# Sixteen modulation slots on GpSimd: scaled and summed over eight chunks there, then added over partitions by TensorE

## The chip, the cores and the metric

The kernel runs on one core of a Trainium2 chip. The metric is the device time of one execution in microseconds (us). Three runs of the kernel before gave 1271.75, 1271.87 and 1272.66 us; the median is 1271.87.

## What is computed

A sequence of 256 tokens with 1024 channels passes two adaptive-norm layers (an "even" mixer with two kinds of attention, an "odd" mixer with banded attention), then two layers of a second block with four mixers and a feed-forward part. The change touches only the modulation of the first two layers:

```
cs = silu(c)                                   # 1024 numbers
for layer in range(2):
    mod = cs @ ada_w[layer] + ada_b[layer]     # 1024 x 3072 matrix
    shift, scale, gate = split(mod, 3)
    h = rms_norm(x, norm_g[layer]) * (1 + scale) + shift
    y = even_mixer(h, ...) if layer == 0 else odd_mixer(h, ...)
    x = x + gate * y
```

So mod is a product of one vector with a matrix of 12.6 MB a layer. Shift and scale of layer 0 are needed before anything else, its gate at the end of the even mixer, shift and scale of layer 1 behind that, and its gate at the end of the odd mixer.

## The kernel before

All weights come as slots of 128 partitions x 2048 float32 (1 MB). NAMES (line 77 on) lists the 200 slots in the order in which TensorE works on them. A ring of four buffers takes most slots, three more buffers in big2 take the modulation slots (line 114 on). SP issues all loads in the order of LOADS (line 138), each behind a wait until the slot that used its buffer before is done (line 1048 on). The transfers that come first are the head: eight modulation slots ada0_0 to ada0_7, for shift and scale of layer 0.

An ordinary slot is a projection of 1024 channels to 256. Its float32 weights are split in two parts: ScalarE copies the rounded high part (L740), VectorE subtracts it (L749, 128x2048, both inputs in SBUF), and TensorE makes three sets of 16 products with them, the third of them with the low part.

A modulation slot (names with "ada") holds 4 chunks of 128 input channels by 512 output channels. TensorE multiplies its 128x128 blocks as the moving operand with cs spread over 32 columns as the stationary one: 16 products a slot, 32 for a pair of slots that shares a PSUM bank. VectorE then picks the columns with four masked reductions (L1887) into mod_raw. Sixteen of the 24 modulation slots come behind the head.

The attention of a layer runs in steps k, with two score maps a step. In each step TensorE makes the scores of pair k, the value products of pair k - 2, the transposes of pair k - 1, and then the slots that the table FILL (line 44) names for that step, whose products keep TensorE occupied while the softmax is made. VectorE adds the bias tables in L578, normalises in L603 (L600 for the second map of a differential head, with two SBUF inputs), subtracts low parts of weights (L749) and of the attention's output (L514), and takes projections out of PSUM. Step 8 and the tail have no scores. Before the change the pairs of modulation slots stand in FILL at steps 0, 2, 3, 5, 8 and the tail of the even layer, in ODD_GATE behind even_out3, and at step 6 of the odd layer.

GpSimd sets some constants at the start and is then idle until the second block (line 2714 on). All instructions of an engine run in its program's order, so a wait of an instruction holds all behind it.

## Time and profile before

| | value |
|---|---|
| median of three runs | 1271.87 us |
| span of the profiled execution, first to last instruction | 1269.9 us |
| TensorE busy | 1245.3 us, 98% |
| VectorE busy | 826.1 us, 65% |
| ScalarE busy | 683.2 us, 54% |
| GpSimd busy | 94.1 us, 7% |
| granted TensorE clock, mean | 0.999 |
| even attention, its eight score steps | 72.2 to 147.2 us |

The profile is that of one execution, recorded in hardware; all times of rows are counted from the start of its span. The span leaves out what lies around the first and the last instruction, so it is 2.0 us below the median of the runs. Busy shares are means over stages with different limits, so single stages are read below.

### The profile page before, as it was taken

What the parts mean: (1) busy time and instruction counts of PE and PEld (TensorE: products, weight loads), DVE (VectorE), ACT (ScalarE), POOL (GpSimd) and SP (SyncE); (2) the same over time, 40 slices, a digit from 0 to 9 for tenths busy, and PEclk for the clock granted to TensorE, in tenths of its full rate; (3) what the DMA queues carried; (4) which work ended last, traced back from release to release, by engine and by line L of the source; (5) the groups of instructions that cost most, each with busy time, mean ns of one, the idle gap of its engine ahead of it and who ended that gap; (6) DMA issues with size and microseconds to landing.
All of it is one profiled execution on the core that took longest, in us unless ns stands there. A gap on an engine that the chain in (4) does not pass through costs nothing.

```text
span 1269.9 us, 24768 instructions
## 1 busy us (share of the span) xinstructions
PE 1245.3 (98%) x10488; PEld 1125.1 (89%) x10488; DVE 826.1 (65%) x1251; ACT 683.2 (54%) x885; POOL 94.1 (7%) x79
## 2 busy tenths in 40 slices
PE   6999999999999999999999999999999999999997
PEld 5998899889999999999888888999999999888886
DVE  3667766886866869766655545766868866655442
ACT  2556446865856567245544435856567345544433
POOL 0000000000001330230000000000330230000000
PEclk9999999999999999999999999999999999999999
DMA  9867665624434433235454554434433225555452
GB/s 386 302 256 271 258 233 197 252 92 167 166 134 166 166 134 133 70 105 195 168 197 170 195 198 167 167 133 167 166 134 109 93 100 189 192 170 195 166 191 75
DMA packets 35102, 222.93 MB, mean 176 GB/s; under 512 B 3888, under 2 KB 8240, under 8 KB 9264
## 3 DMA queue, kind: packets, MB, share of 16 engines
q1 hardware_dynamic: 31248, 216.23, 47.8%
q10 hardware_dynamic: 3744, 5.11, 1.2%
q8 instruction: 83, 1.36, 0.4%
q14 instruction: 27, 0.22, 0.1%
HBM read 220.28 MB, written 1.05 MB: 174 GB/s over the span
## 4 chain that ended last, share of the span: by engine, by line
PE 88%; DVE 5%; ACT 3%; DMA 2%; issue 1%; SPq 0%; ACTq 0%; DVEq 0%
PE pj L635 58%; PE yv L635 14%; PE sc L635 10%; PE tp L635 4%; DVE ring_rounded L749 3%; PE tp L501 1%; DMA ring<-weights 1%; PE tp L1998 1%; ACT w_split L740 1%; DMA xT<-x_t 1%; DVE att_area L578 1%; ACT att_area L532 0%; DVE scr_rounded L2694 0%; DVE xT L1026 0%; ACT hT L2479 0%
## 5 line engine op out<-in xcount | busy, mean ns | idle before, releaser
L749 DVE TENSOR_TENSOR ring_rounded<-ring,w_split 128x2048 fp32r<-128x2048 f32 x106 | 248.5, 2350 | 59.5 <-ACT w_split L740 57.4
L2224 DVE TENSOR_TENSOR ring_rounded<-ring,big_rounded 128x2048 fp32r<-128x2048 f32 x66 | 151.3, 2293 | 107.1 <-ACT big_rounded L2095 107.0
L740 ACT CAST w_split<-ring 128x2048 fp32r<-128x2048 f32 x106 | 202.2, 1907 | 32.1 <-PE pj L635 22.5
L635 PE MATMUL pj<-h_split,w_split 128*128 128x256 f32 x1264 | 172.4, 286 | 0.2 <-ACT w_split L2474 0.2
L635 PE MATMUL pj<-h_split,ring_rounded 128*128 128x256 f32 x1264 | 165.2, 281 | 1.3 <-DVE ring_rounded L749 1.2
L635 PEld LDWEIGHTS pj<-h_split,w_split 128*128 128x128 f32 x1264 | 156.1, 188 | 7.1 <-issue 5.1
L635 PEld LDWEIGHTS pj<-h_split,ring_rounded 128*128 128x128 f32 x1264 | 155.7, 188 | 2.9 <-DVE ring_rounded L749 2.1
L2095 ACT CAST big_rounded<-ring 128x2048 fp32r<-128x2048 f32 x66 | 126.2, 1912 | 49.9 <-PE pj L635 48.3
L635 PE MATMUL pj<-hT_rounded,w_split 128*128 128x256 f32 x1136 | 146.0, 280 | 0.0
L635 PEld LDWEIGHTS pj<-hT_rounded,w_split 128*128 128x128 f32 x1136 | 139.2, 188 | 0.0
L635 PE MATMUL sc<-big_rounded 128*128 128x512 f32 x176 | 68.8, 391 | 0.0
L635 PE MATMUL pj<-big_rounded 128*128 128x512 f32 x176 | 68.5, 389 | 0.0
L1420 POOL TENSOR_TENSOR big<-big 128x512 f32<-128x512 f32 x16 | 30.7, 1920 | 467.6 <-DVE big L1337 459.4
L2324 ACT ACTIVATE big<-pj 128x512 f32<-128x512 f32 x32 | 19.1, 598 | 70.5 <-PE pj L635 70.4
L532 ACT ACTIVATE att_area<-att_area,stat 128x256 f32<-128x256 f32 (+1 forms) x80 | 39.9, 499 | 19.4 <-DVE stat L578 8.3
L2104 ACT CAST big_rounded<-tp 128x512 fp32r<-128x512 f32 x22 | 12.9, 586 | 68.8 <-PE tp L1998 68.8
L635 PE MATMUL yv<-big_rounded,yT_rounded 128*128 128x512 f32 x192 | 49.2, 398 | 0.1
L635 PE MATMUL yv<-big_rounded,rw_rounded 128*128 128x512 f32 x192 | 47.7, 390 | 0.0
L635 PE MATMUL yv<-ring_rounded,yT_rounded 128*128 128x512 f32 x192 | 47.5, 389 | 0.0
L635 PEld LDWEIGHTS yv<-ring_rounded,yT_rounded 128*128 128x128 f32 x192 | 36.0, 188 | 7.5
L635 PEld LDWEIGHTS yv<-big_rounded,rw_rounded 128*128 128x128 f32 x192 | 35.9, 188 | 7.4
L635 PEld LDWEIGHTS yv<-big_rounded,yT_rounded 128*128 128x128 f32 x192 | 35.0, 188 | 8.2 <-issue 0.8
(377 smaller groups left out, 2120.0 us busy)
## 6 DMA issues: line engine op xcount, KB each, us to landing
ring<-weights SPq DMA_DIRECT2D x180, 1024.0 KB, 4.8
big<-weights SPq DMA_DIRECT2D x20, 1024.0 KB, 7.5
first_block<-biases ACTq DMA_DIRECT2D x26, 192.0 KB, 4.4
first_block<-biases SPq DMA_DIRECT2D x6, 192.0 KB, 10.6
xT<-x_t SPq DMA_DIRECT2D x1, 1024.0 KB, 9.3
out_t<-scr SPq DMA_DIRECT2D x4, 256.0 KB, 2.9
con<-constants SPq DMA_DIRECT2D x1, 897.0 KB, 6.5
aux<-small SPq DMA_DIRECT2D x1, 832.0 KB, 10.3
```

What stands on the lines that cost most here:

```text
L501: last = nc.tensor.transpose(tp[m["t"] % 2][:, at:at + P], probs[:, m["g"] % 4, it, jt * P:(jt + 1) * P], C("ident"))
L532: ins = nc.scalar.activation(pr, pr, ACT.Exp, bias=st[:, it:it + 1], scale=-1.0, accum_out=st[:, 2 + it:3 + it])
L578: ins = nc.vector.tensor_tensor_reduce(probs[:, m["g"] % 4, it, 0:size], sc[m["g"] % 2][:, it * SEQ:it * SEQ + size], table[:, P - it * P: ...
L635: return nc.tensor.matmul(out, lhsT, rhs, start=start, stop=stop, skip_group_check=True)
L740: act.post(nc.scalar.copy(w_split[:, w % 2], ring[:, in_ring(idx)]), s["w_high"])
L749: dve.post(nc.vector.tensor_tensor(ring_r[:, at], ring[:, at], w_split[:, w % 2].bitcast(F32), ALU.subtract), s["w_low"])
L1420: pool.tell(nc.gpsimd.tensor_tensor(d, b, b[:, :, n - 1:n].to_broadcast([P, 512 // (2 * n), 2 * n]), ALU.subtract), s["hgrn_diff"])
L1998: last = nc.tensor.transpose(tp[j % 2][:, (2 * c + T) * P:(2 * c + T + 1) * P], by_token(j, T)[:, c * P:(c + 1) * P], C("ident"))
L2095: act.tell(nc.scalar.copy(w_high(i), ring[:, in_ring(w_at(t, i))]), s["ffn_high"])
L2104: act.tell(nc.scalar.copy(hidden_high(j), tp[j % 2][:, :]), s["ffn_placed"])
L2224: dve.tell(nc.vector.tensor_tensor(w_low(t, i), w, value(w_high(i)), ALU.subtract), s["ffn_low"])
L2324: free(act, nc.scalar.activation(GATES[name], b[:, :], ACT.Tanh, scale=0.5), name)
```

## The change

The sixteen slots behind the head no longer go through TensorE as weights. Their layout is changed so that a half slot of 1 MB holds 4 chunks of input channels, with the 512 output channels in order. GpSimd multiplies each chunk (128x512) by its column of cs, and adds the chunks of two half slots in raw, an area that is otherwise used in the second block only. TensorE adds the result over partitions: four products with a 128x128 block of the sum as the stationary operand and one column of ones as the moving one. VectorE copies the four columns out of PSUM. The eight results are called mod0_4, mod0_5, mod1_0 to mod1_5, and stand at other places of FILL than the pairs did. They are no weight slots any more: SP issues their loads behind the streamed weight slots that MOD_AFTER counts, from the fourth on, into the same three buffers, behind a wait on mod_read for the half slot that had the buffer. The sums go round over four places of raw.

```diff
-    "even": {-1: ["even5"], 0: ["even6", "ada0_8", "ada0_9"], 1: ["even8"], 2: ["even13", "ada0_10", "ada0_11"],
-             3: ["even7", "ada1_4", "ada1_5"], 4: ["even9"], 5: ["even10", "ada1_6", "ada1_7"], 6: ["even11"], 7: ["even14"],
-             8: ["ada1_0", "ada1_1"], 9: ["even15"], EVEN_TAIL: ["ada1_2", "ada1_3"]},
-    "odd": {0: ["odd1"], 1: ["odd6"], 2: ["odd2"], 3: ["odd7"], 4: ["odd3"], 5: ["odd8"], 6: ["ada1_10", "ada1_11"],
+    "even": {-1: ["even5"], 0: ["even6"], 1: ["even8", "mod0_4"], 2: ["even13"], 3: ["even7", "mod0_5"], 4: ["even9"],
+             5: ["even10", "mod1_0"], 6: ["even11", "mod1_1"], 7: ["even14"], 8: ["mod1_2"], 9: ["even15"],
+             EVEN_TAIL: ["mod1_3"]},
+    "odd": {0: ["odd1"], 1: ["odd6"], 2: ["odd2"], 3: ["odd7"], 4: ["odd3"], 5: ["odd8"], 6: ["mod1_5"],
             7: ["odd9"]},
-ODD_GATE = ("ada1_8", "ada1_9")
+ODD_GATE = ("mod1_4",)
+MODS = [n for n in NAMES if "mod" in n]
+MOD_AFTER = (3, 4, 6, 7, 8, 9, 10, 11, 12, 13, 14, 15, 17, 18, 19, 20)
+def mod_buffer(j):
+    return RING + (j + 1) % OWN
+        def mod_sum(n):
+            return raw[:, 2 * (n % 4):2 * (n % 4) + 2, 1:SEQ + 1]
+            streamed = [i for i in LOADS if i >= len(HEAD_BUFFERS)]
+            mods_behind = {}
+            for j, n in enumerate(MOD_AFTER):
+                mods_behind.setdefault(streamed[n], []).append(j)
-                sp.dma_start(weights(i), w_d[i]).then_inc(landed[b], 16)
+                sp.dma_start(weights(i), w_d[ROW[i]]).then_inc(landed[b], 16)
+                for j in mods_behind.get(i, ()):
+                    if j < OWN:
+                        before, _ = head_use[mod_buffer(j)]
+                        sp.wait_ge(slot_done, before + 1)
+                    else:
+                        sp.wait_ge(s["mod_read"].sem, j - OWN + 1)
+                    sp.dma_start(mod_weights(j), mod_d[j]).then_inc(landed[mod_buffer(j)], 16)
+        def dve_mod_columns(dve, name):
+            b = done(dve, name)
+            at = 4 * int(name[-1])
+            free(dve, nc.vector.tensor_copy(mod_raw[:, at:at + 4], b[:, 0:4]), name)
+        def pe_mod(pe, name):
+            n = MODS.index(name)
+            use = bank_use(name)
+            pe.eng.wait_ge(bank_free[use % NPJ], use // NPJ)
+            pe.eng.wait_ge(s["mod_read"].sem, 2 * n + 2)
+            for m in range(4):
+                last = matmul(bank_of(name)[:, m:m + 1], mod_sum(n)[:, m // 2, (m % 2) * P:(m % 2 + 1) * P],
+                              C("ones")[:, 0:1], m == 0)
+            last.then_inc(slot_done, 1)
+        def pool_mods(pool):
+            pool.eng.wait_ge(s["cond_ready"].sem, 1)
+            for n, name in enumerate(MODS):
+                if n >= 4:
+                    pool.eng.wait_ge(slot_done, IDX[MODS[n - 4]] + 1)
+                total = mod_sum(n)
+                for half in range(2):
+                    j = 2 * n + half
+                    _, head_uses = head_use[mod_buffer(j)]
+                    pool.eng.wait_ge(landed[mod_buffer(j)], 16 * (head_uses + j // OWN + 1))
+                    w = [mod_weights(j)[:, 2 * k * SEQ:(2 * k + 2) * SEQ] for k in range(4)]
+                    for k in range(4):
+                        ins = nc.gpsimd.tensor_scalar(w[k], w[k], cs[:, 4 * half + k:4 * half + k + 1], None, ALU.mult)
+                    pool.do(ins)
+                    terms = [k.rearrange("p (m t) -> p m t", t=SEQ) for k in w]
+                    if half:
+                        terms = [total] + terms
+                    for k in range(1, len(terms)):
+                        ins = nc.gpsimd.tensor_tensor(total, terms[0] if k == 1 else total, terms[k], ALU.add)
+                        if k < len(terms) - 1:
+                            pool.do(ins)
+                    pool.tell(ins, s["mod_read"])
...
             pool.tell(nc.gpsimd.memset(eps[:, 1:2], 64e-5), s["constants_set"])
+            pool_mods(pool)
             eng.wait_ge(rest_landed, 48)
```

## Rows read from the trace of the kernel before

**Rows 1.** The page, busy time, share of the span and instructions.
```profile
PE 1245.3 (98%) x10488; PEld 1125.1 (89%) x10488; DVE 826.1 (65%) x1251; ACT 683.2 (54%) x885; POOL 94.1 (7%) x79
```

**Rows 2.** The page, shares by engine of the chain that ended last.
```profile
PE 88%; DVE 5%; ACT 3%; DMA 2%; issue 1%; SPq 0%; ACTq 0%; DVEq 0%
```

**Rows 3.** Stretches: length, busy PE, PEld, DVE, ACT, POOL, granted clock, DMA; even steps.
```profile
81.60:89.40 7.80, 7.80 (x68) 7.27 (x64) 6.47 (x23) 4.43 (x11) 0.00 (x0) 1.00 0.97 377
...
129.90:138.20 8.30, 8.30 (x68) 7.65 (x64) 7.42 (x26) 3.58 (x11) 0.00 (x0) 1.00 0.98 379
...
sum 75.00, PE 74.65 PEld 67.17 DVE 57.41 ACT 45.94 POOL 0.00; mean PE 9.33 PEld 8.40 DVE 7.18 ACT 5.74 POOL 0.00
```

**Rows 4.** TensorE in order of time: start, us, line, output and inputs, count, wait before.
```profile
41.70 2.15 PE L635 MATMUL pj<-h_split,ring_rounded 128*128 128x256 f32 x16
...
79.75 1.95 PE L635 MATMUL pj<-big,cs 128*32 128x128 f32 x64
81.63 1.13 PE L635 MATMUL sc<-big 64*128 64x256 f32 x8
...
150.30 1.13 PE L635 MATMUL yv<-probsT,big 128*128 128x256 f32 x4 [0.58 <-ACT probsT L547]
...
189.03 0.50 PE L635 MATMUL tp<-con,rstd 128*128 128x1 f32 x4
189.39 0.91 PE L635 MATMUL sc<-con 128*128 128x128 f32 x6
...
267.55 1.08 PE L635 MATMUL yv<-probsT,big 128*64 128x256 f32 x8 [0.99 <-ACT probsT L547]
```

**Rows 5.** VectorE in order of time, first layer.
```profile
39.35 2.29 DVE L749 TENSOR_TENSOR ring_rounded<-ring,w_split 128x2048 fp32r<-128x2048 f32 x1
...
131.15 0.42 DVE L578 CUSTOM_DVE_ANT_0 att_area<-sc,first_block 128x256 f32<-128x256 f32 x1
...
139.47 0.42 DVE L578 CUSTOM_DVE_ANT_0 att_area<-sc,first_block 128x256 f32<-128x256 f32 x1 [0.28 <-DVE big L1862]
...
190.12 0.19 DVE L1887 CUSTOM_DVE_ANT_0 diag<-pj,con 128x32 f32<-128x32 f32 x1
...
190.36 0.19 DVE L1887 CUSTOM_DVE_ANT_0 diag<-pj,con 128x32 f32<-128x32 f32 x1
```

**Rows 6.** VectorE by source line: least, median and most ns of one.
```profile
L603 DVE TENSOR_SCALAR att_area<-att_area,stat x72: 285/354/357, 77.7 to 870.5; 128x256 f32<-128x256 f32 x64, 128x128 f32<-128x128 f32 x8
```

**Rows 7.** GpSimd in order of time, second block.
```profile
429.27 0.99 POOL L1435 TENSOR_TENSOR big<-big 128x256 f32<-128x256 f32 x1 [6.07 <-issue]
430.34 1.43 POOL L1420 TENSOR_TENSOR big<-big 128x512 f32<-128x512 f32 x1
...
445.69 2.98 POOL L1420 TENSOR_TENSOR big<-big 128x512 f32<-128x512 f32 x1
```

**Rows 8.** VectorE in order of time, the same stretch.
```profile
416.22 0.69 DVE L1689 TENSOR_TENSOR big<-raw 128x512 f32<-128x512 f32 x1
...
429.70 1.11 DVE L1689 TENSOR_TENSOR big<-raw 128x512 f32<-128x512 f32 x1
430.85 1.73 DVE L1691 SCALAR_TENSOR_TENSOR raw<-big,vec,raw 128x256 f32<-128x256 f32 x2
...
445.06 2.71 DVE L749 TENSOR_TENSOR ring_rounded<-ring,w_split 128x2048 fp32r<-128x2048 f32 x1
447.69 1.26 DVE L1367 COPY vfirst<-raw 128x512 f32<-128x512 f32 x1
```

**Rows 9.** GpSimd by source line: least, median and most ns of one.
```profile
L1970 POOL TENSOR_TENSOR big<-big x16: 1263/1277/3220, 535.8 to 1023.6; 128x512 f32<-128x512 f32 x16
...
L1407 POOL CAST att_area_rounded<-con x8: 293/368/462, 282.7 to 549.9; 128x128 fp32r<-128x128 f32 x8
```

**Rows 10.** SP's queue in order of time: the issue of loads.
```profile
21.01 6.39 SPq L1058 DMA_DIRECT2D ring<-weights  x4
...
99.73 0.43 SPq L1058 DMA_DIRECT2D ring<-weights  x1
```

More of the change, by code:

```diff
@@ L105, in is_split @@
 def is_split(name):
-    return not any(part in name for part in ("ada", "branch1", "ffn", "down"))
+    return not any(part in name for part in ("ada", "mod", "branch1", "ffn", "down"))
 SPLIT = [i for i, n in enumerate(NAMES) if is_split(n)]
@@ L136 @@
 BUFFERS = buffers()
+ROW = {i: row for row, i in enumerate(i for i, b in enumerate(BUFFERS) if b)}
 EARLY_BY = 6
-LOADS = sorted(range(len(NAMES)), key=lambda i: (max(BUFFERS[i][2], i - EARLY_BY if i >= len(HEAD_BUFFERS) else -1), i))
+LOADS = sorted((i for i, b in enumerate(BUFFERS) if b),
+               key=lambda i: (max(BUFFERS[i][2], i - EARLY_BY if i >= len(HEAD_BUFFERS) else -1), i))
 in_ring = lambda idx: BUFFERS[idx][0]
@@ L632, in weights, with mod_weights @@
             return ring[:, b] if b < RING else big2[:, (b - RING + 1) * SLOT:(b - RING + 2) * SLOT]
+        head_use = {}
+        for i_, b_ in enumerate(HEAD_BUFFERS[:BUFFERS.index(None)]):
+            head_use[b_] = (i_, BUFFERS[i_][1])
+        def mod_weights(j):
+            at = (mod_buffer(j) - RING + 1) * SLOT
+            return big2[:, at:at + SLOT]
+        def mod_sum(n):
+            return raw[:, 2 * (n % 4):2 * (n % 4) + 2, 1:SEQ + 1]
         def matmul(out, lhsT, rhs, start=True, stop=True):
@@ L2309, in act_slot @@
                 act_diff_root(act)
-            if "ada" not in name:
+            if "ada" not in name and name not in MODS:
                 act_highs(act, split_beyond(name.split(".")[0],
@@ L2329, in dve_slot @@
         def dve_slot(dve, name):
-            if "." not in name and "ada" not in name:
+            if "." not in name and "ada" not in name and name not in MODS:
                 dve_lows(dve, split_beyond(name, 1))
@@ L2334, in dve_evacuate @@
         def dve_evacuate(dve, name):
-            if "ada" in name:
+            if name in MODS:
+                dve_mod_columns(dve, name)
+            elif "ada" in name:
                 if ada_part(name) % 2:
@@ L2767, in pack_weights @@
         for n in range(4):
-            out[IDX[f"{t}branch{n}"]] = a["w_branch_2"][layer, n].reshape(2, P, D).transpose(1, 0, 2).reshape(P, SLOT)
+            out[ROW[IDX[f"{t}branch{n}"]]] = a["w_branch_2"][layer, n].reshape(2, P, D).transpose(1, 0, 2).reshape(P, SLOT)
         put(a["w_out_2"][layer], numbered(t + "out", 4))
@@ L2773, in pack_weights, with pack_modulations @@
         for i in range(FC):
-            out[IDX[f"{t}ffn{i}"]] = slots[i]
+            out[ROW[IDX[f"{t}ffn{i}"]]] = slots[i]
         slots = a["w_ffn_down_2"][layer].reshape(FC // 2, 2, P, D).transpose(0, 2, 1, 3).reshape(FC // 2, P, SLOT)
         for i in range(FC // 2):
-            out[IDX[f"{t}down{i}"]] = slots[i]
+            out[ROW[IDX[f"{t}down{i}"]]] = slots[i]
     return out
+def pack_modulations(a):
+    parts = np.stack([a["ada_w"][layer].reshape(2, 4, P, 6, 4 * P).transpose(3, 0, 2, 1, 4).reshape(6, 2, P, SLOT)
+                      for layer in range(2)])
+    return np.concatenate([parts[int(n[3]), int(n[-1])] for n in MODS])
 def pack_vectors(a):
@@ L2819 @@
         "weights": pack_weights(a),
+        "modulations": pack_modulations(a),
         "vectors": pack_vectors(a),
```

23 lines of the change are left out of this document (13 added, 10 removed).

## The prediction

> **What bounds the kernel now.** I read the shares of the span by engine first, then the chain of work that ended last, then single stretches. TensorE is busy for 98% of the span, GpSimd for 7% [rows 1], and the chain of waits names TensorE for 88% of its length [rows 2]. So time that leaves TensorE is worth its full length, if the engine behind it is not late. The table by attention step of the even layer says where that holds: TensorE is full at full clock, VectorE works 6.47 of 7.80 us in an early step and 7.42 of 8.30 in a later one, in all eight steps 57.41 of 75.00 us [rows 3]. In that later step its first instruction starts at 131.15, and the next step's at 139.47 after an idle time of 0.28 us that an instruction of VectorE itself ended [rows 5]: 8.04 us of work in a step of 8.3 of TensorE's. VectorE is the second bound, 0.3 us below the first.
>
> **What is removed.** A pair of modulation slots is 32 products, twice the 16 of a slot: the row "x64" at 79.75 counts their two passes and spans 1.95 us, 1.88 net of the overlap with the next row, which starts at 81.63 [rows 4]. Eight such pairs go. Not each is worth 1.88 us:
> - Behind even6, even13, even7 and even10 TensorE has no wait after the pair. Four times 1.88 = 7.5 us. The pair at the tail of the even attention: 1.9 us.
> - The pair of step 8 (from 147.8 to 149.7) is followed by the product over probsT at 150.30, which waited for ScalarE [rows 4]. Only this cover goes, so 0.
> - The pair behind even_out3 lies beside the residual and the squares that its successors need anyway, so 0 on TensorE. On VectorE four masked reductions stand from 190.12 on ahead of the scaled norm, at a pitch of 0.235 us [rows 5]: 0.94 us, for one copy of four columns instead, which I put at 0.2 (one reduction on 32 columns takes 0.19). 0.75 us.
> - In the odd attention TensorE waits 0.99 us for ScalarE soon after the pair, at 267.55 [rows 4]. Again VectorE's 0.75 counts.
> Sum 10.9 us.
>
> **What is added on TensorE.** Four products of one column a pair. The nearest row, four of 128x1 at 189.03, spans 0.50, 0.36 net of its successor at 189.39 [rows 4]. Five of the eight lie on the path: 1.8 us; the others fall into the waits above. Net 9.1 us saved, if nothing else happens.
>
> **What is added on GpSimd.** Sixteen half slots of four tensor_scalar 128x512 and three or four adds 128x512. An add takes 1.277 us in the median and 1.263 at least [rows 9], with its wait on the one before about 1.36. A tensor_scalar of that size is in no row. From below: a cast of a quarter of the columns takes 0.293 at least [rows 9], so not less than that. From above: the add, 1.28, which reads two inputs. I take 0.65: half of the add, one input being half of two, and between a cast's least time and twice its median of 0.368. A half slot is then 4 x 0.65 + 3.5 x 1.36 = 7.4 us, all 118 us.
>
> The Trainium skill, "GPSIMD Engine Reference", section "When to use GPSIMD", says that two-input elementwise work there is about half as fast as on VectorE and one-input work near line rate. The trace agrees on the first, 1.277 us against VectorE's 0.69, and no run here shows the second. By that page the tensor_scalar would take about what VectorE takes for an operation of 512 columns, 0.69, and the sum would stand; it speaks against rival 2.
>
> **What GpSimd does to VectorE.** This decides. At 429.27 GpSimd starts a tensor_tensor of 0.99 us, at 429.70 VectorE one of 128x512 with both inputs in SBUF. It takes 1.11 us instead of the 0.69 of the same line at 416.22, so it ends at 430.81. GpSimd's next (430.34) ends at 431.77, and the two VectorE instructions behind take 1.73 instead of 1.0 [rows 7, 8]. At 445.69 GpSimd's lasts 2.98, across a split subtraction that itself lasts 2.71 for 2.29; then the copy of SBUF to SBUF, 128x512, lasts 1.26 [rows 7, 8]. So the two engines exclude each other for whole instructions and take turns. The wait of VectorE behind a waiting GpSimd add is 0.75 us, since 0.3 of the add's 1.27 passes before it needs the turn. Behind a tensor_scalar of 0.65 it would be 0.2 to 0.25. With a gap of 0.2 us in between both lose 0.2. A mean over the mix (half and half) is 0.5 back to back, 0.33 behind a gap, and 0.38 for an instruction that meets GpSimd at a random point.
>
> Which VectorE instructions count? Subtractions of split weights (L749), those at L600, L514 and L1016 have two SBUF inputs. The normalisation at L603 has one: 0.354 us for 128x256 [rows 6], below the 0.42 of L578 for the same size, which reads PSUM [rows 5], so it runs in a faster mode. That the copy at 447.69, which has one SBUF input too, was held speaks for counting it, and I do.
>
> Rule by rule: the Trainium skill, "SBUF — State Buffer", section "SBUF: two separate sides", says that VectorE and GpSimd share one port pair as an exclusive lock that is held for an instruction, and that a VectorE instruction takes it with two SBUF inputs or in a two-port mode. The rows at 429 to 448 agree, 1.11 for 0.69 us. By the rule L603 counts.
>
> Without L603 the waits of the eight steps, summed below, are 4 x 0.4 + 4 x 1.8 = 8.8 instead of 19.2 us and fit into VectorE's idle time but for 1.5; with 2.5 at the start and 1 behind, 5.0 us are lost and the time would be 1268. That is the other end of this choice.
>
> **Is GpSimd busy when VectorE needs the turn?** The first of its loads stands behind even1's, and the four ring loads with even1's among them are issued between 21.0 and 27.4 us [rows 10], so it lands near 34. From then a half slot arrives with about every streamed weight slot, every 6 to 10 us. With one turn of 2.0 us for L749 and short ones for the rest, a half slot takes 9.6 us. So GpSimd stays behind its loads and works without a pause until about 150 us. TensorE's deadlines hold: half slot 11 is done at about 150, and mod1_3 stands at 151 plus what VectorE loses. On SP's queue a load of a half slot waits for mod_read (the one three before is read), and the weight slots behind it wait too, some up to 10 us: even10's is issued at 99.73 [rows 10] and its products start at 122.1, once the step's other products behind 119.6 are done, 22 us of cover, so no loss. Were GpSimd slower, both covers would be gone, see the rivals.
>
> **The sum of the waits.**
> - Start: from 34 to 42 us the first half slot meets eight L2604 and the L749 of 39.35, which ends at 41.64. TensorE takes its result at 41.70 [rows 4, 5], so all waits ahead of it count: five turns, about 2.5 us.
> - The eight steps: an early step (0 to 3) has L749 and four L603, 0.38 + 0.33 + 0.5 + 0.33 + 0.5 = 2.0 us of waits; a later one (4 to 7) L749, two L603, one small tensor_scalar, two L600 and one L514, 2.8 us. Together 4 x 2.0 + 4 x 2.8 = 19.2. VectorE's own time is 57.4 [rows 3] less 4 x 0.75 for the reductions, and 0.03 us between each of some 170 instructions, 5 us: 59.5. With the waits 78.7. TensorE needs 75.0 - 4 x 1.88 + 4 x 0.36 = 68.9. Excess 9.8 us. About 0.7 of the idle time lies where it can't be used, and 2.0 are made good behind step 7, where VectorE has less to do. 8.5.
> - Behind the attention: the last four half slots end near 187 us, beside L749, L514 and L2616, three turns: 1.5. The eight L1016, from 194 us on, are just clear.
>
> Sum 12.5 us. With the 9.1 saved that is +3.4. The profiled span is 1269.9 and the median of the runs 1271.87, so 2.0 us lie around the span: 1273.3 and 2.0, forecast 1275.3.
>
> **The rivals.**
> 1. The waits find idle time. For it: VectorE idles 1.3 us of 7.8 early [rows 3], the score and probability buffers are two and four deep, and no row shows a tensor_scalar held. Against: the 0.28 us of idle time [rows 5]. At its full size 9.1 us stay saved, 1263; without L603 it is the 1268 above.
> 2. GpSimd is slow (slower than before clearly): its tensor_scalar costs as much as an add, 1.28. A half slot is 10.2, with its turns 12.6 us; the turns cost VectorE 3.3 and 4.3 instead of 2.0 and 2.8 a step, 30.4 over the eight, so 19.7 are lost there, 3.5 at the start and 2 behind: 25.2 in place of 12.5, 1288. From about 1.1 us a tensor_scalar on, half slot 11 (180 us) also misses mod1_3 (171), where TensorE stands in order with even_out behind it: 9 us more, 1297. For it: the cast of only 128 columns takes up to 0.46 [rows 9]. Against: its least, 0.293.
> 3. The loads: a mod_read wait on SP holds even10 to even15 back until ScalarE's split is late. Each half slot over 10 us adds its excess, five times 2, so 1285. Against: the 22 us of cover [rows 10].
>
> **Chances.** The forecast 0.43, with its own range 1269 to 1283; rival 1 0.28; rival 2 0.23; rival 3 0.05; 0.01 for something unseen. Within 0.2% (2.5 us, about what a measurement of this kernel tells from no change) lies 0.16 of the forecast's 0.43 and 0.01 of rival 1; 0.27 of rival 1 is faster, and 0.01 of the forecast. Faster 0.28, same 0.17, slower 0.55 with rivals 2 and 3. Range 1262 to 1293: all of rival 1, and two thirds of rival 2.
>
> **What would show it.** L749 in 75 to 150 us with a mean over 2.5 instead of 2.29 us, and L603, L600 above 0.5: right. L603 at 0.354 beside a busy GpSimd: wrong in its count. GpSimd's tensor_scalar near 0.65 us, its last add before 190 us. An interval between two score products of steps 5 to 7 of over 9.5 us: VectorE is the bound. TensorE idle before mod1_3 because of GpSimd: rival 2. Granted clock still 1.00, as in rows 3. If the attention steps shrink by 1.5 us each where a pair left, the forecast is wrong and rival 1 right.

## The result, and the profile after

The changed kernel takes 1314.51 us in the median of 4 runs (1314.33 to 1315.61), the kernel before, on the same chip, 1272.05. The ratio is 1.0337, with a 95% interval of 1.0325 to 1.0349: 42.5 us slower, where 3.4 slower was forecast and 1293 was the upper end of the range. The profiled execution took 1315.6 us, its span 1313.6. Line numbers moved, those that are read here mostly by 11 to 23: L658 is TensorE's product (L635 before), L772 the subtraction of split weights (L749), L614 the normalisation (L603), L611, L525 and L1039 were L600, L514 and L1016, L763 is ScalarE's split (L740 before).

The page of the kernel after, its busy times, the slices for GpSimd and the granted clock, and the chain that ended last; they answer to [rows 1, 2]:

```profile
PE 1253.7 (95%) x10040; PEld 1132.5 (86%) x10040; DVE 836.6 (64%) x1195; ACT 682.5 (52%) x885; POOL 297.4 (23%) x199
...
POOL 0799999500000231150000000000330230000000
PEclk9998869999999999999999999999999999999999
...
PE 79%; POOL 11%; DVE 3%; DMA 2%; ACT 2%; issue 1%; SPq 0%; ACTq 0%; POOLq 0%; DVEq 0%
```

GpSimd is now 11% of the chain, where it had no entry. It works without a pause from 40.8 to 250 us, and within that time, from about 100 to 200 us, TensorE's granted clock falls (each digit of these two lines is a slice of 33 us, in tenths). The stretches say where the time went. In each row: length, busy PE, PEld, DVE, ACT, POOL, granted clock, DMA share and rate. First the kernel before: from the first to the eighth score product of the even attention, its end and tail, even_out, the norm with the first odd projections.

```profile
72.20:138.20 66.00, 65.65 (x725) 58.82 (x724) 49.40 (x151) 40.46 (x82) 0.00 (x0) 1.00 0.69 265
138.20:160.00 21.80, 21.22 (x265) 19.28 (x264) 16.50 (x36) 11.69 (x21) 0.00 (x0) 1.00 0.63 241
160.00:185.80 25.80, 25.80 (x224) 25.08 (x219) 14.92 (x32) 12.28 (x13) 0.00 (x0) 1.00 0.62 237
185.80:209.50 23.70, 23.70 (x252) 22.87 (x251) 17.40 (x31) 11.39 (x16) 0.00 (x0) 1.00 0.46 162
```

The same four stretches of the kernel after:

```profile
72.80:150.60 77.80, 66.39 (x503) 59.21 (x502) 56.48 (x120) 39.85 (x82) 75.53 (x47) 0.91 0.56 199
150.60:197.30 46.70, 24.85 (x153) 22.20 (x152) 18.34 (x32) 13.64 (x22) 45.19 (x31) 0.70 0.56 211
197.30:225.50 28.20, 28.20 (x218) 27.66 (x218) 16.86 (x24) 10.29 (x11) 27.44 (x17) 0.90 0.47 184
225.50:249.80 24.30, 23.03 (x196) 22.19 (x194) 17.70 (x24) 11.39 (x16) 23.64 (x13) 1.00 0.44 157
```

The losses are 11.8, 24.9, 2.4 and 0.6 us; 0.6 came before the first of these stretches, and 0.6 in the odd attention and the projections behind it. That is 41.0 of the 43.7 us by which the spans differ. The other 2.7 come in the second block, where both kernels do the same: 0.5 by 400 us of the kernel before, 0.9 near 515 and 1.4 near 1000 us; why is open. In the second stretch TensorE is busy for 24.85 of 46.70 us, so 21.3 of the 24.9 lost are waits; the other 3.6 are longer busy time, with fewer products than before, at a granted clock of 0.70. TensorE in order of time, with the wait before an instruction in brackets, to set beside [rows 4]:

```profile
107.59 0.95 PE L658 MATMUL pj<-con,raw 128*128 128x1 f32 x8
...
112.82 1.97 PE L658 MATMUL yv<-probsT,big 128*64 128x256 f32 x8 [3.22 <-ACT probsT L558]
...
140.44 2.04 PE L658 MATMUL yv<-probsT,big 128*128 128x256 f32 x4 [4.84 <-DVE big L1896]
...
161.81 1.88 PE L658 MATMUL yv<-probsT,big 128*128 128x256 f32 x4 [2.96 <-ACT probsT L558]
...
171.66 1.84 PE L658 MATMUL pj<-con,raw 128*128 128x1 f32 x8 [7.12 <-POOL raw L1963]
...
174.85 3.98 PE L658 MATMUL pj<-h_split,w_split 128*128 128x256 f32 x16
...
195.69 1.84 PE L658 MATMUL pj<-con,raw 128*128 128x1 f32 x8 [11.78 <-POOL raw L1963]
```

The last two bracketed rows are mod1_2 and mod1_3, which wait 18.9 us for GpSimd's adds. The clock is low behind these waits: sixteen projection products took 3.98 us, which take 2.15 in other rows, and the granted clock of 161.8 to 197.3 is 0.60 of the higher level, 2.4 GHz, as a mean over stretches at both levels. GpSimd by source line (least, median and most ns, then the first and last start in us):

```profile
L1957 POOL TENSOR_SCALAR big<-big,cs x64: 1557/1563/3757, 40.8 to 238.5; 128x512 f32<-128x512 f32 x64
```

```profile
L1963 POOL TENSOR_TENSOR raw<-raw,big x48: 1175/1188/3336, 52.2 to 247.0; 128x512 f32<-128x512 f32 x48
```

A tensor_scalar of 128x512 takes 1.56 us at its best, 1.83 in the mean. GpSimd's last add ends at 250.1, so a half slot takes (250.1 - 40.8) / 16 = 13.1 us. And the first starts at 40.8, when its load lands, not at 34. What that does on the other queues: SP's queue (start, length of the issue), then ScalarE, then VectorE:

```profile
99.27 0.33 SPq L1092 DMA_DIRECT2D big<-modulations  x1
99.64 0.43 SPq L1085 DMA_DIRECT2D ring<-weights  x1
110.90 0.33 SPq L1092 DMA_DIRECT2D big<-modulations  x1
111.27 0.43 SPq L1085 DMA_DIRECT2D ring<-weights  x1
```

```profile
106.85 1.91 ACT L763 CAST w_split<-ring 128x2048 fp32r<-128x2048 f32 x1 [7.51 <-DMA ring<-weights]
...
108.66 0.50 ACT L543 ACTIVATE att_area<-att_area,stat 128x256 f32<-128x256 f32 x1
...
156.14 1.92 ACT L763 CAST w_split<-ring 128x2048 fp32r<-128x2048 f32 x1 [7.16 <-DMA ring<-weights]
```

```profile
122.37 0.17 DVE L605 RECIPROCAL stat<-stat 128x2 f32<-128x2 f32 x1 [3.93 <-ACT att_area L543]
```

VectorE's normalisation, by source line (to set beside [rows 6]):

```profile
L614 DVE TENSOR_SCALAR att_area<-att_area,stat x72: 285/354/1317, 78.4 to 912.8; 128x256 f32<-128x256 f32 x64, 128x128 f32<-128x128 f32 x8
```

Its most is 1317 ns where it was 357. From 84 us on a load of modulations goes out every 11 to 16 us, when GpSimd has read a half slot, and a ring load stands right behind most of them. The one at 99.64 is that of slot even9: ScalarE's split waits 7.5 us for it, and the exponentials of the step (L543) stand behind the split in ScalarE's order; VectorE's reciprocal and TensorE's yv wait for those. In the kernel before, even9's load was issued at 82.21, and the split of even10, whose load went at 99.73 [rows 10], ran at 109.64:

```profile
82.21 0.64 SPq L1058 DMA_DIRECT2D ring<-weights  x1
```

```profile
109.64 1.90 ACT L740 CAST w_split<-ring 128x2048 fp32r<-128x2048 f32 x1
```

### The profile page after: what moved, and what is told of

The parts are those of the page before. It is cut to its first block, busy times and chain, and to the rows that moved or that the text cites. A ratio compares the mean times of both kernels' runs of the same rounds, so it can differ in the third digit from the quotient of the medians.

```text
span 1313.6 us, 23952 instructions
## 1 busy us (share of the span) xinstructions
PE 1253.7 (95%) x10040; PEld 1132.5 (86%) x10040; DVE 836.6 (64%) x1195; ACT 682.5 (52%) x885; POOL 297.4 (23%) x199
## 4 chain that ended last, share of the span: by engine, by line
PE 79%; POOL 11%; DVE 3%; DMA 2%; ACT 2%; issue 1%; SPq 0%; ACTq 0%; POOLq 0%; DVEq 0%
PE pj L658 52%; PE yv L658 13%; PE sc L658 9%; POOL big L1957 7%; POOL raw L1963 5%; PE tp L658 4%; DMA ring<-weights 1%; DVE ring_rounded L772 1%; DMA big<-modulations 1%; PE tp L2073 1%; PE tp L512 1%; ACT att_area L543 0%; DVE att_area L589 0%; DVE hT_rounded L1039 0%; ACT w_split L763 0%
## 5 line engine op out<-in xcount | busy, mean ns | idle before, releaser
L772 DVE TENSOR_TENSOR ring_rounded<-ring,w_split 128x2048 fp32r<-128x2048 f32 x106 | 249.8, 2362 | 59.6 <-ACT w_split L763 57.5
L763 ACT CAST w_split<-ring 128x2048 fp32r<-128x2048 f32 x106 | 202.2, 1908 | 69.9 <-DMA ring<-weights 36.3
L658 PE MATMUL pj<-h_split,w_split 128*128 128x256 f32 x1264 | 175.6, 290 | 0.2 <-ACT w_split L2553 0.2
L658 PE MATMUL pj<-h_split,ring_rounded 128*128 128x256 f32 x1264 | 165.5, 281 | 1.7 <-DVE ring_rounded L772 1.6
L658 PEld LDWEIGHTS pj<-h_split,w_split 128*128 128x128 f32 x1264 | 159.3, 192 | 7.2 <-issue 5.1
L658 PEld LDWEIGHTS pj<-h_split,ring_rounded 128*128 128x128 f32 x1264 | 155.9, 188 | 3.2 <-DVE ring_rounded L772 2.5
L658 PE MATMUL pj<-hT_rounded,w_split 128*128 128x256 f32 x1136 | 146.7, 281 | 0.2 <-DVE hT_rounded L1039 0.2
L658 PEld LDWEIGHTS pj<-hT_rounded,w_split 128*128 128x128 f32 x1136 | 139.8, 189 | 0.4 <-DVE hT_rounded L1039 0.4
L1957 POOL TENSOR_SCALAR big<-big,cs 128x512 f32<-128x512 f32 x64 | 116.2, 1832 | 40.6 <-DMA big<-modulations 39.1
L1963 POOL TENSOR_TENSOR raw<-raw,big 128x512 f32<-128x512 f32 x48 | 72.0, 1500 | 3.8
L658 PE MATMUL sc<-big_rounded 128*128 128x512 f32 x176 | 68.8, 391 | 0.0
L658 PE MATMUL pj<-big_rounded 128*128 128x512 f32 x176 | 68.5, 389 | 0.0
L658 PE MATMUL yv<-big_rounded,yT_rounded 128*128 128x512 f32 x192 | 49.2, 398 | 0.1
L658 PE MATMUL yv<-big_rounded,rw_rounded 128*128 128x512 f32 x192 | 47.7, 390 | 0.0
L658 PE MATMUL yv<-ring_rounded,yT_rounded 128*128 128x512 f32 x192 | 47.5, 389 | 0.0
L543 ACT ACTIVATE att_area<-att_area,stat 128x256 f32<-128x256 f32 (+1 forms) x80 | 39.8, 498 | 10.7 <-ACT att_area L543 3.3
L658 PEld LDWEIGHTS yv<-ring_rounded,yT_rounded 128*128 128x128 f32 x192 | 36.0, 188 | 7.5
## 6 DMA issues: line engine op xcount, KB each, us to landing
first_block<-biases SPq DMA_DIRECT2D x6, 192.0 KB, 12.5
```

Source lines behind the costliest of these rows:

```text
L543: ins = nc.scalar.activation(pr, pr, ACT.Exp, bias=st[:, it:it + 1], scale=-1.0, accum_out=st[:, 2 + it:3 + it])
L658: return nc.tensor.matmul(out, lhsT, rhs, start=start, stop=stop, skip_group_check=True)
L763: act.post(nc.scalar.copy(w_split[:, w % 2], ring[:, in_ring(idx)]), s["w_high"])
L772: dve.post(nc.vector.tensor_tensor(ring_r[:, at], ring[:, at], w_split[:, w % 2].bitcast(F32), ALU.subtract), s["w_low"])
L1957: ins = nc.gpsimd.tensor_scalar(w[k], w[k], cs[:, 4 * half + k:4 * half + k + 1], None, ALU.mult)
L1963: ins = nc.gpsimd.tensor_tensor(total, terms[0] if k == 1 else total, terms[k], ALU.add)
```

## The experiments

Theory A: the loss is GpSimd's pace. Its 13 us a half slot hold TensorE at mod1_2 and mod1_3, and through SP's queue the weights, ScalarE's split and the exponentials. Theory B: the loss is the port that GpSimd and VectorE share, by the turns that VectorE waits for. Times are medians of 4 to 10 runs (e6 ran once), each beside the kernel before on the same chip (1271.8 to 1272.1).

| kernel | us | ratio to before, 95% |
|---|---|---|
| before | 1271.9 | |
| after | 1314.5 | 1.0325 to 1.0349 |
| e1_no_arithmetic | 1270.9 | 0.9981 to 1.0000 |
| e2_ports_only | 1286.1 | 1.0096 to 1.0126 |
| e8_tensor_waits | 1318.4 | 1.0353 to 1.0384 |
| e9_load_waits | 1311.3 | 1.0291 to 1.0322 |
| e3_no_scale | 1274.7 | 1.0010 to 1.0041 |
| e6_forms | 1273.7 | one run |
| e7_wide | 1322.8 | 1.0386 to 1.0421 |
| e10_spread | 1299.6 | 1.0202 to 1.0236 |
| e12_spread_ports | 1300.4 | 1.0206 to 1.0240 |
| e13_short_ports | 1280.1 | 1.0049 to 1.0079 |
| e14_spread_short | 1312.5 | 1.0306 to 1.0340 |
| e11_filled | 1268.3 | 0.9964 to 0.9984 |

**The change without its arithmetic.** In pool_mods:

```diff
-                    for k in range(4):
-                        ins = nc.gpsimd.tensor_scalar(w[k], w[k], cs[...], None, ALU.mult)
...
-                        ins = nc.gpsimd.tensor_tensor(total, ..., terms[k], ALU.add)
+                    ins = nc.gpsimd.memset(total[:, :, 0:1], 0.0)
                     pool.tell(ins, s["mod_read"])
```

> GpSimd leaves out all scaling and adding (it writes one column of the sum and posts mod_read when a half slot has landed); loads, products and their order stay. Theory A (GpSimd's own pace, 12 to 14 us a half slot, holds the loads on SP's queue and TensorE's products) and theory B (the turns that GpSimd takes from VectorE make the time) both expect 1264 to 1269: by the sum of the prediction with 0.88 us for the four products that the profile after shows, 10.9 - 5 x 0.88 = 6.5 us below 1272. Theory C (the placing of loads and products by itself costs most of the 42 us) expects over 1290.

1270.9 us, slower than both theories expected (1264 to 1269) and far from theory C. All that the change costs is GpSimd's arithmetic: 1314.5 - 1270.9 = 43.6 us. But with the arithmetic left out the change brings 1 us, and the interval ends at no change at all, not the 9.1 of my sum.

**Port turns alone.** The same 120 instructions work on an area that nobody uses, each product behind the one before it, and GpSimd waits only for the first landing. SP's loads wait only for landings and TensorE's products for nothing:

```diff
-                        sp.wait_ge(s["mod_read"].sem, j - OWN + 1)
+                        sp.wait_ge(landed[mod_buffer(j)], 16 * (head_uses + j // OWN))
...
-            pe.eng.wait_ge(s["mod_read"].sem, 2 * n + 2)
+            pe.eng.wait_ge(s["mod_read"].sem, 1)
...
-                    w = [mod_weights(j)[...] for k in range(4)]
+                    w = [flat(vfirst)] * 4
```

> GpSimd makes all 64 tensor_scalar and 56 adds of the changed kernel on an area that nobody else uses, from the landing of the first half slot on, and nobody waits for it: SP waits for landings instead of mod_read, TensorE reads a constant sum. So only the turns at the shared port stay. Theory A expects 2 to 12 us above e1_no_arithmetic, 1268 to 1278. Theory B expects nearly the changed kernel's time, over 1300.

1286.1, 8 above A's range and 14 below B's: turns alone cost 15.2 us over e1, and nobody waits for GpSimd. VectorE's busy time grows from the 821.0 us of e1 to 854.0. In the kernel after it is 836.6, 15.6 over e1 and not 33.0. So the 15.2 are the price of turns where nothing else holds the engines; how much of the 43.6 is turns, they do not say.

**Each of the two waits alone.** On top of the kernel with turns alone, GpSimd waits for each landing and counts its half slots on mod_read again, and either TensorE waits for the count (e8) or SP's loads do (e9).

> Left out: GpSimd's scaling and adding is done on an unused area, so the modulation is not the reference's. GpSimd does the same instructions on VectorE's port and posts each half slot when it has landed and its sums are done; TensorE's four products wait for that, as in the changed kernel; SyncE's loads wait only for landings, never for GpSimd. So the price of TensorE's own waits is measured on top of the port turns (1286.1 with nobody waiting). Theory A (GpSimd's pace does its harm through SyncE's queue: weights late, ScalarE's split late, exponentials late): at step 5 to 8 of the even attention nothing more is lost, and mod1_2 and mod1_3 still wait, some 7 and 12 us in the changed kernel, less here because the attention is not late and GpSimd has had no less time: the half slots for mod1_3 end at about 41 + 12 x 13.5 = 203 us against a request at 170 or so. That is 15 to 28 us for both together: 1301 to 1314. Theory A2 (both waits count, and hide one another): 1306 to 1314 here and nearly as much with the loads' waits alone. Theory B (port turns alone): 1284 to 1290.

> Left out: as in the kernel with TensorE's waits alone, the scaling and adding is done on an unused area. Here SyncE's modulation loads wait for GpSimd's count as in the changed kernel, and TensorE's products do not. Theory A: the weight loads behind each held load keep GpSimd's pace, the split of ScalarE waits 4 to 7 us for them at slots 92 to 169 us, and the attention's steps after 108 us take 11 to 14 us: the attention ends 10 to 15 us late, and even_out too: 1296 to 1306. Theory A2: each of the two waits alone gives 80% of the whole, 1306 to 1312. Theory B: 1284 to 1290, with no wait of ScalarE's split on a DMA above 2 us.

TensorE's waits alone give 1318.4 us, the loads' alone 1311.3, both together (the kernel after) 1314.5. So the two hide one another, as A2 says; they don't add. A2 had 1306 to 1312 for the loads' waits and is met; for TensorE's it had 1306 to 1314, and e8 is 4 above that. In e8 GpSimd starts 1.0 us later than in the kernel after and loses another 3.2 over twelve half slots, which are the 4.2 us by which mod1_3 starts later. With the loads free, ScalarE's split waits nowhere for a DMA between 85 and 175 us, and TensorE waits for GpSimd at four pairs instead of two. TensorE in e8:

```profile
127.85 1.02 PE L658 MATMUL pj<-con,raw 128*128 128x1 f32 x8 [1.91 <-POOL raw L1964]
...
151.91 1.84 PE L658 MATMUL pj<-con,raw 128*128 128x1 f32 x8 [12.71 <-POOL raw L1964]
...
199.85 1.84 PE L658 MATMUL pj<-con,raw 128*128 128x1 f32 x8 [12.82 <-POOL raw L1964]
```

mod1_3 starts at 199.85 here and at 195.69 in the kernel after: the same wall, GpSimd's twelfth half slot. In e9, without TensorE's waits, ScalarE shows the other chain:

```profile
106.85 1.90 ACT L763 CAST w_split<-ring 128x2048 fp32r<-128x2048 f32 x1 [7.65 <-DMA ring<-weights]
```

**What the forms cost.** Each half slot of this kernel does another form, nothing else.

> A measurement: GpSimd makes other instructions on each half slot (its sums are left out): tensor_scalar by a column of 256 columns, by a constant, not in place, of 2048 columns, a copy, a product of two tensors with the column spread over 512, the same over four chunks at once, an add of 1024 columns. If the column operand costs the 1.56 us, the constant takes 0.6 to 0.8; if the instruction is slow in every form, the constant takes 1.5 as well, and the product of two tensors, 1.2 to 1.3, is the faster way to scale. Its time itself should be near e1_no_arithmetic plus what the turns cost, 1265 to 1280.

GpSimd in order of time (start, total length, form, count):

```profile
48.62 7.62 POOL L1963 TENSOR_SCALAR big<-big 128x512 f32<-128x512 f32 x4 [0.80 <-DMA big<-modulations]
...
70.96 4.04 POOL L1972 TENSOR_TENSOR big<-big,cs 128x512 f32<-128x512 f32 x4 [3.44 <-DMA big<-modulations]
```

The first row is longer than a later one of its form (5.87 for four). At their shortest a tensor_scalar takes 0.94 for 256 columns and 1.56 for 512, by a column and not in place, and 1.47 by a constant; a copy takes 0.60. So it is neither the column nor the place: the tensor_scalar is slow in every form. The product with a column spread along the row takes 1.01, as in the last row: two inputs, and faster than the form with one.

**One wide product.** The scaling as one product of 128x2048 with spread columns, then one add of 1024 columns and one or two of 512, 3 or 4 instructions a half slot; nothing is left out.

> The changed kernel with the same results, but a half slot is one product of two tensors of 128x2048 (the columns spread), one add of 1024 columns, and one or two of 512, in place of four tensor_scalar and three or four adds. Estimate from rows: 4.5 + 2.3 + 1.2 (+ 1.2) = 8 to 9.2 us instead of 11 to 12. Theory A: the twelfth half slot is done 12 x 3 = 30 us earlier, 1280 to 1292. Theory B: GpSimd holds its turn for up to 4.5 us at once, so no gain, 1310 to 1325.

1322.8, the slowest of all, though GpSimd is busy with it for 152 us only, against 203 in the kernel after. VectorE's busy time is 893.3 and the normalisation takes 1214 ns in the mean between 60 and 300 us. TensorE waits nowhere for GpSimd. Two normalisations of VectorE in this kernel, which take 0.7 undisturbed:

```profile
113.99 5.86 DVE L614 TENSOR_SCALAR att_area<-att_area,stat 128x256 f32<-128x256 f32 x2
```

GpSimd's product of 3.60 us from 113.68 on and its add of 2.34 behind it lie across the two. Theory A in its simple form falls here: a shorter half slot does not help if its instructions are long. B's range holds the time.

**The spread product, instructions as short as before, and its turns alone.**

```diff
-                        ins = nc.gpsimd.tensor_scalar(w[k], w[k], cs[:, 4 * half + k:4 * half + k + 1], None, ALU.mult)
+                        column = cs[:, 4 * half + k:4 * half + k + 1].to_broadcast([P, 2 * SEQ])
+                        ins = nc.gpsimd.tensor_tensor(w[k], w[k], column, ALU.mult)
```

> The same result as the reference. The scaling by tensor_scalar is written as a two-tensor product with the column spread along the row, 128x512 each: 1.01 us in the run of the forms, against 1.56, with the instructions as short as before. Theory A (GpSimd's pace): a half slot falls from 10.4 us of its own to 4 x 1.02 + 3.5 x 1.18 = 8.2, with turns some 10.5 to 11 instead of 13.5: the last half slot for mod1_3 ends about 35 us earlier, and most of the 28 us of waits go: 1290 to 1300. Theory B (the turns on the port are the bulk, as the wide product showed): the product with two tensors holds the port for its whole length as well, and the time stays at 1308 to 1320.

> Left out: the arithmetic is done on an unused area and nobody waits for it, so the modulation is not the reference's. GpSimd's instructions are those of the kernel with the spread column (1299.6): 64 two-tensor products and 56 adds of 128x512. The kernel with tensor_scalar in their place, nobody waiting, took 1286.1: 15.2 above the one with no arithmetic, for 120 instructions. Theory P (VectorE loses by turn, one turn an instruction of GpSimd, whatever its length): 120 turns again, 1284 to 1287; then 13 to 16 us of the spread kernel's 28.7 are turns and the rest its waits. Theory L (VectorE loses by the length that GpSimd holds the port): own length falls from 10.4 to 8.2 us a half slot, the price to 12: 1281 to 1284. If it is over 1290, the spread product hurts VectorE more than tensor_scalar does.

e10, with nothing left out, takes 1299.6 us, 15 less than the kernel after, as A expected. One wait of TensorE for GpSimd is left in it, and none of ScalarE's split for weights:

```profile
176.08 1.02 PE L658 MATMUL pj<-con,raw 128*128 128x1 f32 x8 [3.60 <-POOL raw L1964]
```

But e12, where nobody waits, takes 1300.4. So turns alone are enough for its whole loss, and both theories of e12 fall: the same number of instructions, the products shorter than the tensor_scalar, costs the kernel 29.5 us over e1 instead of 15.2. The fine order of time shows why. In e2, beside tensor_scalar, a row of VectorE and the row of GpSimd across it, and one pair beside an add:

```profile
199.68 0.47 DVE L1039 SCALAR_TENSOR_TENSOR hT_rounded<-hT,mod,h_split 128x256 fp32r<-128x256 f32 x1
...
200.87 2.28 DVE L772 TENSOR_TENSOR ring_rounded<-ring,w_split 128x2048 fp32r<-128x2048 f32 x1
...
231.73 1.16 DVE L614 TENSOR_SCALAR att_area<-att_area,stat 128x256 f32<-128x256 f32 x1
```

```profile
198.36 2.00 POOL L1957 TENSOR_SCALAR vfirst<-vfirst,cs 128x512 f32<-128x512 f32 x1
...
200.46 4.05 POOL L1957 TENSOR_SCALAR vfirst<-vfirst,cs 128x512 f32<-128x512 f32 x1
...
231.45 1.28 POOL L1965 TENSOR_TENSOR raw<-raw,vfirst 128x512 f32<-128x512 f32 x1
```

Beside GpSimd's tensor_scalar VectorE keeps its times (0.47 and 2.28) and GpSimd's instruction stretches from 1.56 to 2.00 and 4.05. Beside its tensor_tensor the next normalisation takes 1.16 for 0.35. In e12 GpSimd's spread products (212.6 to 217.3 us) and adds, before and behind them, run across the same eight L1039:

```profile
L1039 DVE SCALAR_TENSOR_TENSOR hT_rounded<-hT,mod,h_split x8: 953/1258/1402, 211.9 to 220.1; 128x256 fp32r<-128x256 f32 x8
```

In e2 the median of these is 0.475. They stand on the path of the odd layer's first projections, whose products wait 4.0 us for them. It isn't absolute: beside a tensor_scalar one L1039 of e2 took 0.83, and a short L595 0.59 instead of 0.23.

**Shorter instructions, nobody waiting.** As e2, each instruction cut in two of 128x256.

> Left out: as in the kernel with nobody waiting and tensor_scalar (1286.1). Here each of GpSimd's instructions is cut into two of 128x256 (0.94 us against 1.56 in the run of the forms; an add some 0.65 against 1.2), so there are 240 in place of 120 and the total length is 10 to 20% more. Theory T (a VectorE instruction waits for the rest of the one that holds the port, so shorter ones cost it less each time but are met more often): the mean of the normalising tensor_scalar falls from 628 ns to 500, the price from 15.2 to 8 to 12: 1279 to 1283. Theory P (a price by the turn): twice as many turns, 20 to 30 us: 1291 to 1301. Theory L (by the length held): 16 to 19 us: 1287 to 1290.

1280.1, 9.2 us of turns instead of 15.2, the normalisation 515 ns between 60 and 260 us where e2 has 696: Theory T. Twice the meetings, half the wait, and GpSimd pays: it works until 325 us, 18 us a half slot instead of 14. By the medians of its rows 32 of its 52 us more are the short instructions' own length.

**The adds alone.**

> Left out: the scaling by the condition's columns; the adds, all loads and all waits are those of the changed kernel. A half slot is 3.5 adds, 4.1 us of its own and 5 to 6.5 with turns, in place of 12 to 14. Theory A (of the 43.6 us over the kernel with no arithmetic 28 are waits for GpSimd's pace and 15 its turns on the port): no load and no product waits for GpSimd, and 56 instructions of 120 are left to take turns: 7 us, 1276 to 1280. Theory B (the waits come from the loads in SyncE's order whatever the pace): 1290 or more, with ScalarE's split waiting over 4 us for weights.

1274.7, but the ten runs spread from 1271.1 to 1281.8, and the trace is that of the fastest. Below A's range by 1.3, far from B's: in that trace GpSimd works for 5.1 us a half slot, no split waits for weights and no product for GpSimd. The waits belong to the pace and not to the order of the loads.

**Both remedies.** The spread product, and every product and add cut in two, with the waits of the change and nothing left out.

> The same result as the reference: the scaling by a two-tensor product with the column spread along the row, and every product and every add cut into two of 128x256. The kernel with whole ones took 1299.6, and the same instructions with nobody waiting 1300.4, so its 28.7 us over the kernel with no arithmetic (1270.9) are turns on the port. Theory T (each meeting costs VectorE the rest of the instruction that holds the port, so half the length costs half): cutting brings the turns to 13 to 17 us, and a half slot has about 0.6 us more of its own (some 10 with gaps), so mod1_3 still waits 2 to 4 us: 1285 to 1291. Rival (a price by the meeting): 1300 or more. Neither sees it below 1280, so not below the kernel before.

1312.5, a miss by over 20 us. VectorE did get its time back (busy 842.5, e10 868.7), and then GpSimd fell back to 12.7 us a half slot (40.6 to 243.7), and the old waits returned. TensorE:

```profile
167.59 1.84 PE L658 MATMUL pj<-con,raw 128*128 128x1 f32 x8 [6.92 <-POOL raw L1966]
...
191.24 1.84 PE L658 MATMUL pj<-con,raw 128*128 128x1 f32 x8 [12.37 <-POOL raw L1966]
```

I had counted on a half slot of some 10 us. GpSimd's product by source line, in e10, then in e14:

```profile
L1958 POOL TENSOR_TENSOR big<-big,cs x64: 1032/1041/3101, 40.7 to 212.8; 128x512 f32<-128x512 f32 x64
```

```profile
L1959 POOL TENSOR_TENSOR big<-big,cs x128: 607/612/2695, 40.6 to 232.9; 128x256 f32<-128x256 f32 x128
```

Two halves take 1.22 us where the whole takes 1.04, and two halves of an add 1.44 where the whole takes 1.20. Over the sixteen half slots that is 24.6 us by the medians (17.1 by the least times), and GpSimd's busy time on them grows by 24.7, from 172.9 to 197.6. So GpSimd did not lose at the port what VectorE won there: it is late by the short instructions' own length, of which I had counted 0.6 us a half slot and which is 1.1 to 1.5.

**Where the gain of the empty kernel went.** e1 with thirteen 128x128 products into unused columns where the pair of the odd step 6 had been:

```diff
+            if name == "mod1_5":
+                for m in range(13):
+                    last = matmul(bank_of(name)[:, P:2 * P], C("ident"), C("ones"))
```

> Left out: the scaling and adding of GpSimd altogether, as in the kernel with no arithmetic (1270.9). Added: at the odd attention's step 6, where the pair of modulation slots was taken away, thirteen 128x128 products into unused columns of the same bank, some 1.8 us, about what the removed pair took. Theory C (the removed pair stood before a wait for the exponentials, 2.1 us there without it, and TensorE's clock fell behind that wait): the 2.9 us lost at that step come back, no lower clock in the rows behind it: 1267.5 to 1269.5. Rival (the loss there belongs to ScalarE or to the loads, and does not depend on what TensorE does): 1270.5 to 1273.

1268.3, 2.6 us below e1 in the medians, though the two intervals overlap by a little. Theory C's time is met, but the traces bear out only its mechanism. TensorE in e1, then in e11:

```profile
264.48 1.08 PE L658 MATMUL yv<-probsT,big 128*64 128x256 f32 x8 [2.08 <-ACT probsT L558]
265.50 1.66 PE L512 MATMUL tp<-con,att_area 128*128 128x128 f32 x8
266.80 3.25 PE L658 MATMUL pj<-h_split,w_split 128*128 128x256 f32 x16
```

```profile
261.85 3.15 PE L658 MATMUL pj<-con 128*128 128x128 f32 x26
264.93 1.13 PE L658 MATMUL sc<-big 64*128 64x256 f32 x8
265.99 1.08 PE L658 MATMUL yv<-probsT,big 128*64 128x256 f32 x8
267.01 1.09 PE L512 MATMUL tp<-con,att_area 128*128 128x128 f32 x8
267.86 2.13 PE L658 MATMUL pj<-h_split,w_split 128*128 128x256 f32 x16
```

Without the pair TensorE waits 2.08 us, and the next rows run at the lower level: 1.66 for 1.09, 3.25 for 2.13, granted clock 0.91 of the higher level over 262 to 280 us (1.00 in e11). The thirteen added products make 26 passes and take 3.08 us net, not the 1.8 expected. With them there is no wait; yv starts 1.5 us later than in e1, and the next group behind these rows starts at 269.82 instead of 269.89, in a kernel that had been 0.65 us behind e1 before the step. So the added work is free, and removing the pair had brought nothing. It does not bring 2.9 us: over this step e1's lead on the kernel before shrinks by 0.6 us (3.1 to 2.5) and e11's grows by 0.2 (2.4 to 2.6). The rest of the difference between the two appears near 515 us (1.1) and near 1000 us (1.1), in code that is the same in both. There e1 loses 1.1 and 1.2 us on the kernel before, as the kernel after does (0.9 and 1.4), and e11 does not. That is not explained; e1's ten runs spread over 2.7 us themselves.

## Why the prediction was wrong

The sign was right and the size wrong by a factor of twelve. By its own steps:

1. "What is removed", 10.9 us, and "added on TensorE", five times 0.36. The products span 0.95 us, 0.88 net (107.59 to 108.47): the four make eight passes, counted x8, where my row at 189.03 was four passes, which I had read as four products. That takes 5 x 0.52 = 2.6 off the 9.1. The rest is read from e1's lead on the kernel before: 5.2 us gained up to the seventh score product (4.9 ahead at 129.89, from 0.3 behind at the first), 0.8 lost by the eighth, 1.5 lost at step 8, where I had 0 (a wait of 1.66 us, then a row of 1.84 us for 1.13), 0.5 gained at the tail, where I had 1.5, and nothing at the two places where I counted VectorE's reductions for 0.75 each. 2.5 us ahead at 300 us in place of 9.1, and the two places of the second block take 2.3 of that in the profiled run (1271.7). "Granted clock still 1.00" was wrong. The odd step 6, put at 0 for TensorE, was right within 0.6.
2. **The step that failed first: the price of GpSimd's tensor_scalar.** I took 0.65 us, between 0.293 and 1.28. It is 1.56, above my upper bound: "one input being half of two" has it the wrong way round, since the two-input product takes 1.01. With the later start (40.8, not 34), a half slot of 13.1 instead of 9.6 us puts the twelfth at 195.6 us, not 150. TensorE asked for it at 183.9, which I had at 151 plus VectorE's losses. "TensorE's deadlines hold" fails with it. By the Trainium skill, "GPSIMD Engine Reference", section "When to use GPSIMD", one-input work runs near line rate; the measured 1.56 us contradicts it for tensor_scalar, against the 0.69 that VectorE takes for two inputs of that size, and the copy's 0.60 agrees.
3. **The second: "no loss" on SP's queue.** I counted 22 us of cover from even10's issue to its product. The nearest consumer is ScalarE's split, ahead of the exponentials of its step in order. In the kernel before, even10's split runs 9.9 us behind the issue of its load (99.73 to 109.64). In the kernel after even9's load goes at 99.64, 17 us later than before, even10's at 111.27, and even9's split waited 7.5 us. e9 shows that this way alone, with the turns, gives 40 us over e1. Rival 3 named the mechanism and priced it at 1285 with chance 0.05.
4. Turns on the port. The mechanism is there: the rows at 231 us show a normalisation held for 0.8 us, so L603 was rightly counted (0.81 us; I had 0.75 behind an add), and L772's mean of 2375 ns and the normalisation's 730 between 75 and 150 us bear on my signs: that for the normalisation, over 500, is met, that for L749, over 2.5 us, is not. The sign for VectorE as the bound came too, 11.7 us between score products of steps 5 and 6 (122.75 to 134.47), but VectorE was not the bound: around that step it waited 3.9 and 4.1 us for ScalarE's exponentials. The Trainium skill, "SBUF — State Buffer", section "SBUF: two separate sides", agrees with these rows for tensor_tensor; a lock held for a whole instruction is not what the 2.28 us of L772 inside GpSimd's 4.05 shows for tensor_scalar. The size, 12.5 against the 15.2 of e2, was close by luck, since two errors work against each other: GpSimd works for 1.4 times as long as I had it (until 250 us, not 187), and the half of its instructions that are tensor_scalar hardly hold VectorE.
5. Rival 2, GpSimd slow, was the case that came, with mod1_3 missed. It was priced at 1288 to 1297, since I took the wait at mod1_3 for 9 us; it is 7.1 and 11.8 at two pairs. By the rival's own half slot of 12.6 us the twelfth would have ended at 34 + 12 x 12.6 = 185 us, not 180, so that slip took 5 off it. Its upper bound on the tensor_scalar was the add, and the loads' wait was kept apart as another rival, although both follow from the same slow half slot.

So of the 43.6 us of the arithmetic, 15.2 come with turns alone and nobody waiting (e2); the other 28 come only once something waits for GpSimd's pace, by either of two ways that cover each other (e8, e9). Open: how far turns and waits overlap within the kernel after, where VectorE's busy time grows only half as much as in e2; the 2.7 us lost in the second block; and why GpSimd's tensor_scalar lets VectorE pass.

## What to carry to other kernels

Before work moves to another engine, find its first consumer in every queue behind each new wait, and let the price of one unmeasured operation run through all the deadlines at once: one slow half slot made the products, the loads and the exponentials late. Price GpSimd's work beside a busy VectorE from both sides, since each way tried here relieved one and slowed the other: fewer and wider instructions (e7) and the faster product (e10) shortened GpSimd's work and held VectorE longer, and cutting the instructions in two gave VectorE its time back and made GpSimd's work longer (e14). No form tried beats the pair's 1.88 us on TensorE, and there was little to win: even with no arithmetic the change brought 1 us, and 3.7 with added products. Work that stands before a wait is worth nothing to remove, as 3.1 us of added products that cost nothing showed: look for the wait behind it, and at the clock behind that.

## What the runs showed of the hardware that I had not expected

- GpSimd, 128x512 f32: tensor_scalar 1.56 us, two-input product with a spread column 1.01 to 1.04, add 1.18, copy 0.60 (e6, and the add in the kernel after). For 128x256: tensor_scalar 0.94, product 0.61, add 0.63 to 0.73 (e6, e13, e14). Two halves take longer than the whole, 1.22 against 1.04 us for the product.
- Beside VectorE the two kinds behave differently: a tensor_scalar of GpSimd stretches (1.56 to 4.05 us in e2) and VectorE mostly keeps its time; a tensor_tensor of GpSimd holds VectorE for its rest (0.35 to 1.16 us in e2, L1039 from 0.475 to 1.258 in e12).
- The same arithmetic with 3 or 4 long instructions a half slot cost 23 us more than with 7 or 8 short ones (1322.8 against 1299.6).
- After most of TensorE's waits of 2 us and more the rows show the lower clock level, 1.2 GHz, for some microseconds: 3.98 instead of 2.15 us for sixteen products, clock 0.60 over the 35.5 us around mod1_2 and mod1_3. At 1.7 us it went either way: the yv of 1.13 us behind such a wait took 1.84 in e1 and 1.13 in e3.
